# Latent attention of one layer: the order of block 0's key squares, the latent reads and block 1's query transpositions

## The chip, the cores and the metric

The kernel runs on one core of a Trainium2 chip. The metric is device time in microseconds (us), the median of several executions. The core has a matrix engine (TensorE, PE in the rows), a vector engine (VectorE, DVE), a scalar engine (ScalarE, ACT), a general engine (GpSimd, POOL) and a sequencer that issues transfers (SyncE, SP). Each works through its own queue in order; they wait for each other by semaphores. TensorE multiplies out of on-chip memory (SBUF) into accumulation banks (PSUM), which VectorE and ScalarE read here.

## The reference, cut to what matters

The network computes, for 256 tokens of width 1024: feed-forward, SSM layer, feed-forward, feed-forward, **latent attention**, feed-forward, short convolution, and a stick-breaking attention. All is float32; the kernel multiplies large matrices as three products of high and low parts. Only the latent attention is touched here:

```python
def mla_mixer(h, positions, w_in, q_a_norm, kv_a_norm, w_q_b, w_kv_b, q_norm, k_norm, w_out):
    proj = h @ w_in                                      # 384 + 256 + 32 columns
    cq   = rms_norm(proj[..., :Q_LORA], q_a_norm)
    ckv  = rms_norm(proj[..., Q_LORA:Q_LORA + KV_LORA], kv_a_norm)
    k_rope = proj[..., Q_LORA + KV_LORA:]
    q  = (cq @ w_q_b).reshape(b, s, 16, 64 + 32)         # queries
    kv = (ckv @ w_kv_b).reshape(b, s, 16, 64 + 64)       # keys and values
    ...                                                  # rms_norm of q_nope, q_rope, k_nope, k_rope
    q_rope, k_rope = apply_rope(...)                     # rotation by position
    o = causal_block_attention(q_nope, q_rope, k_nope, k_rope, v)   # blocks of 128 queries
    return o.reshape(b, s, 16 * 64) @ w_out
```

## The kernel before, in words

Tokens stand in two blocks of 128 (`tb` 0 and 1). Weights come in units of up to 128 x 2048 elements through a ring of four slots: SyncE loads a unit when the low part of the unit four before it is done (`lo_ready`), ScalarE rounds its high part (`w_hi`, L1297), VectorE subtracts for the low part (`w_lo`, L1864), TensorE multiplies. `split_to(n)` in an engine's program does all units up to n at this place of its queue; `split_half` does half of a low part (L1882). In the latent attention `u0` is the first unit: u0+6 and u0+7 hold the key/value weights, u0+8 to u0+11 the output weights, and u0+12 on belong to the next layer.

The stages of each block are these. `block(...)` (L950) is a product of one 512-column stretch into one accumulation bank; banks are used in turn, so a block waits until the one four before it is read (`claim`). ScalarE reads the query banks (`read_q`) and squares them (`square_q`), VectorE sums the squares (`q_means`), ScalarE takes the root (`root`), VectorE inverts and scales (`inverse`, `scale_q`); GpSimd rotates the last 32 columns of each head (`rotate`), the last two steps behind the squares. Keys and values are read into `kv_tok` (`read_kv`, on ScalarE, two of them on VectorE), squared (`square_k`), summed (`k_means`), and GpSimd takes a power of the sums (L2655) and scales the keys (L2656). `means_ready` counts VectorE's sums in their order.

Then TensorE transposes queries and keys, four heads at a time (`token_turn`, a "turn"; L618 in the rows). All turns of the layer are numbered by the list `MLA_TURNS` and use two banks alternately, so a turn waits until the turn two before it has been copied out (`claim_turn`); `read_turn` on ScalarE or VectorE is this copy. A round of attention (`mla_round`) is four heads of block 0 or two of block 1: `scores` (L1022, with a mask L1024), `tops` (the maximum, VectorE), `exps` (ScalarE), `weights_turn` and its copy `read_weights`, `values` (L1041), `out_norm` (VectorE), and per two rounds an output turn (`out_turn`), whose high and low parts feed the output product.

The order of all this is written out by hand, one list for each engine, and the engines' lists have to agree. Before, TensorE turned all eight groups of queries and then the four key groups of block 0 ahead of `scores(0)`.

## Time and profile before

| | us |
|---|---|
| median of 3 runs | 1321.52 |
| lowest, highest | 1317.18, 1322.16 |
| the profiled execution | 1323.06 |
| its span, first to last instruction | 1321.3 |
| TensorE busy in it | 1292.5 |
| VectorE busy | 767.4 |
| ScalarE busy | 681.8 |
| GpSimd busy | 120.5 |

The part of the latent attention that the change touches lies at about 843 to 882 us of the span. The mean granted clock of TensorE over the span was 0.993 of full speed. A busy share is the time in which an engine has an instruction under way; a row of a timeline begins with its start in us from the span's start and its duration, "x8" is eight instructions merged, and the bracket is the time for which the engine stood still before it and who ended that.

### The profile page before, as it was taken

How to read it: one execution, taken by the hardware profiler on the slowest of the kernel's cores; microseconds unless marked ns; L12 is line 12 of the kernel's file. 1: busy time of each engine (PE TensorE's matmuls, PEld its weight loads, DVE VectorE, ACT ScalarE, POOL GpSimd, SP SyncE). 2: the span in 40 equal slices, each digit the busy share in tenths (PEclk: the TensorE clock that was granted, in tenths of full speed). 3: DMA queues.
4: the chain of work that ended last, by engine and by line, in shares of the span. 5: the costliest groups of instructions: out<-in, count | busy, mean ns of one | idle time of the engine just before them, and what ended most of it. 6: DMA issues, size and time to landing. Idle time of an engine off the chain costs nothing.

```text
span 1321.3 us, 18338 instructions
## 1 busy us (share of the span) xinstructions
PE 1292.5 (98%) x6930; PEld 1103.6 (84%) x6930; DVE 767.4 (58%) x912; ACT 681.8 (52%) x926; POOL 120.5 (9%) x198
## 2 busy tenths in 40 slices
PE   8999999999999999999999999989999999999997
PEld 6888889999778888888888888778888888998895
DVE  5555645778676555554555544865655545766663
ACT  6454435678775544442544534854645434443552
POOL 3000000007630000000000001620000000000000
PEclk9999999999899999999999999999999999999999
DMA  9556645543227455565555563423556564766401
GB/s 295 191 190 207 212 142 191 161 159 96 96 96 254 153 187 181 183 219 160 190 179 183 180 211 120 144 64 96 186 178 198 186 225 125 194 190 223 157 4 48
DMA packets 180478, 219.81 MB, mean 166 GB/s; under 512 B 8666, under 2 KB 132895, under 8 KB 180415
## 3 DMA queue, kind: packets, MB, share of 16 engines
q1 hardware_dynamic: 179438, 218.01, 50.7%
q8 instruction: 42, 0.69, 0.2%
q10 hardware_dynamic: 688, 0.79, 0.2%
q0 software_dynamic: 288, 0.15, 0.1%
q14 instruction: 22, 0.17, 0.0%
HBM read 217.87 MB, written 1.05 MB: 166 GB/s over the span
## 4 chain that ended last, share of the span: by engine, by line
PE 88%; DVE 6%; ACT 5%; issue 1%; DMA 0%; SPq 0%; DVEq 0%; POOLq 0%; ACTq 0%; POOL 0%
PE acc L601 27%; PE acc L603 26%; PE acc L602 26%; PE tr L618 3%; DVE w_lo L1864 2%; ACT w_hi L1297 1%; PE tr L903 1%; PE aux L1041 1%; PE acc L1022 1%; ACT xT_hi L1310 1%; DMA raw<-in_ffn_w_gate 0%; ACT R_hi L1496 0%; DVE zn L2412 0%; PE acc L1238 0%; DVE zr L2411 0%
## 5 line engine op out<-in xcount | busy, mean ns | idle before, releaser
L1864 DVE TENSOR_TENSOR w_lo<-raw,w_hi 128x2048 fp32r<-128x2048 f32 (+1 forms) x196 | 440.7, 2276 | 180.4 <-ACT w_hi L1297 180.3
L1297 ACT ACTIVATE w_hi<-raw 128x2048 fp32r<-128x2048 f32 (+1 forms) x198 | 369.2, 1899 | 118.9 <-PE acc L603 118.1
L601 PE MATMUL acc<-w_hi,xT_hi 128*128 128x512 f32 (+1 forms) x914 | 363.4, 398 | 4.5 <-DVE w_lo L2472 2.8
L603 PE MATMUL acc<-w_hi,xT_lo 128*128 128x512 f32 (+1 forms) x914 | 355.7, 389 | 0.0
L602 PE MATMUL acc<-w_lo,xT_hi 128*128 128x512 f32 (+1 forms) x914 | 355.2, 389 | 0.0
L601 PEld LDWEIGHTS acc<-w_hi,xT_hi 128*128 128x128 f32 x914 | 172.3, 189 | 40.3 <-issue 4.9
L603 PEld LDWEIGHTS acc<-w_hi,xT_lo 128*128 128x128 f32 x914 | 172.2, 188 | 36.4
L602 PEld LDWEIGHTS acc<-w_lo,xT_hi 128*128 128x128 f32 x914 | 172.5, 189 | 33.2
L601 PE MATMUL acc<-w_hi,hT_hi 128*128 128x512 f32 x448 | 175.8, 392 | 0.4 <-DVE y_sb L2382 0.4
L603 PE MATMUL acc<-w_hi,hT_lo 128*128 128x512 f32 x448 | 174.5, 390 | 0.0
L602 PE MATMUL acc<-w_lo,hT_hi 128*128 128x512 f32 x448 | 174.4, 389 | 0.0
L601 PE MATMUL acc<-xT_hi,w_hi 128*128 128x256 f32 (+1 forms) x592 | 167.1, 283 | 1.2 <-DVE w_lo L1864 0.6
L602 PE MATMUL acc<-xT_lo,w_hi 128*128 128x256 f32 (+1 forms) x592 | 165.9, 281 | 0.0
L603 PE MATMUL acc<-xT_hi,w_lo 128*128 128x256 f32 (+1 forms) x592 | 165.9, 281 | 0.0
L2007 DVE SCALAR_TENSOR_TENSOR h<-acc,rstd,sg 128x256 f32<-128x256 f32 x88 | 38.6, 479 | 165.8 <-ACT sg L1400 165.8
L1400 ACT ACTIVATE sg<-acc,rstd 128x256 f32<-128x256 f32 x88 | 37.0, 472 | 181.9 <-PE acc L603 181.8
L601 PEld LDWEIGHTS acc<-xT_hi,w_hi 128*128 128x128 f32 (+1 forms) x592 | 112.2, 190 | 2.0 <-issue 1.8
L602 PEld LDWEIGHTS acc<-xT_lo,w_hi 128*128 128x128 f32 (+1 forms) x592 | 112.2, 190 | 0.3
L603 PEld LDWEIGHTS acc<-xT_hi,w_lo 128*128 128x128 f32 (+1 forms) x592 | 112.2, 190 | 0.0
L2533 POOL TENSOR_SCALAR mean_square<-square_sum 128x1 f32<-128x1 f32 x18 | 5.0, 275 | 1040.4 <-ACT junk L1347 574.0
L601 PEld LDWEIGHTS acc<-w_hi,hT_hi 128*128 128x128 f32 x448 | 84.1, 188 | 17.8 <-DVE y_sb L2382 0.8
L603 PEld LDWEIGHTS acc<-w_hi,hT_lo 128*128 128x128 f32 x448 | 84.1, 188 | 17.8
(294 smaller groups left out, 1140.7 us busy)
## 6 DMA issues: line engine op xcount, KB each, us to landing
raw<-in_ffn_w_down SPq DMA_DIRECT2D x88, 512.0 KB, 4.7
raw<-in_ffn_w_gate SPq DMA_DIRECT2D x87, 512.0 KB, 4.2
raw<-in_ffn_w_up SPq DMA_DIRECT2D x87, 512.0 KB, 5.6
raw<-in_ssm_w_in SPq DMA_DIRECT2D x48, 512.0 KB, 4.7
raw<-in_w_in_a SPq DMA_DIRECT2D x64, 256.0 KB, 4.0
raw<-in_ssm_w_out SPq DMA_DIRECT2D x16, 512.0 KB, 4.0
raw<-in_mla_w_out SPq DMA_DIRECT2D x8, 512.0 KB, 4.6
raw<-in_w_out_a SPq DMA_DIRECT2D x8, 512.0 KB, 4.8
```

What stands on the lines that cost most here:

```text
L601: pe.matmul(o, lh, rh, start=start, stop=False, skip_group_check=skip)
L602: pe.matmul(o, lh, rl, start=False, stop=False, skip_group_check=skip)
L603: return pe.matmul(o, ll, rh, start=False, stop=stop, skip_group_check=skip)
L618: last = pe.transpose(tr[0:n, k % 2, at:at + P], src, ident[:])
L903: last = pe.matmul(tr[:, k % 2, tb * GW + r * HP:tb * GW + (r + 1) * HP], E[:, tb, r * P:(r + 1) * P], xdt[:, g % 2, tb, r * HP:(r + 1) * ...
L1022: pe.matmul(o[:, j * w:(j + 1) * w], qT[0:QK, h0 + j, tb * P:(tb + 1) * P], kT[0:QK, h0 + j, 0:w], start=j == 0, stop=False, skip_group_ch ...
L1041: last = pe.matmul(aux[:, r % 2, j * (VD + 1):(j + 1) * (VD + 1)], pT[:, r % 2, at:at + P], kv_tok[:, kb, h0 + j, NOPE:], start=kb == 0, s ...
L1297: inst = act.activation(w_hi[:, u % RING, 0:n], raw[:, u % RING, 0:n], ACT.Copy)
L1310: inst = act.activation(dst, tr[:, k % 2, at:at + P], ACT.Copy, scale=scale)
L1400: act.activation(sg[:, tb, :], bank(p0 + n, tb)[:, 0:CW], ACT.Silu, scale=rstd[:, tb:tb + 1]).then_inc(gated, 1)
L1864: inst = dve.tensor_tensor(w_lo[:, u % RING, 0:n], raw[:, u % RING, 0:n], w_hi[:, u % RING, 0:n].bitcast(F32), ALU.subtract)
L2007: acc_free(dve.scalar_tensor_tensor(h[:, tb, :], bank(p0 + n, tb)[:, CW:2 * CW], rstd[:, tb:tb + 1], sg[:, tb, :], ALU.mult, ALU.mult), p0 ...
```

## The change

Six things change, all in the latent attention. (1) ScalarE reads all eight key/value banks; VectorE's `read_kv` is gone. (2) ScalarE does the high part of unit u0+8 before the key/value reads, then block 0's key squares, then block 1's query squares (the query squares stood first before, the key squares eleven steps later). VectorE sums block 0's key squares ahead of block 1's query squares, GpSimd finishes block 0's keys before it copies block 1's rotated keys, and the numbers that they wait for in `means_ready` follow. (3) TensorE turns block 0's queries between block 1's key/value blocks, has no turns of block 1's queries there, starts `scores(0)` behind the third key turn, and turns block 1's queries behind the four rounds of scores: two before the weights' turns, one after `values(0)`, one after `values(1)`. (4) The third query turn of block 1 is copied by ScalarE instead of VectorE. (5) VectorE's low part of unit u0+8 is done in two halves, around `out_norm(0)`. (6) ScalarE's high part of unit u0+9 stands behind `read_weights(2)`, ahead of the read of the last query turn.

```diff
--- before.py
+++ after.py
@@ -147,9 +147,9 @@
 SUM_PAIR = (19, 20)
 MLA_TURNS = {name: n for n, name in enumerate(
     [("p", tb, j) for tb in range(TB) for j in range(2)]
-    + [("q", tb, quad) for tb in range(TB) for quad in range(4)]
+    + [("q", 0, quad) for quad in range(4)]
     + [("k", 0, quad) for quad in range(4)]
-    + [("t", 0), ("t", 1), ("t", 2), ("k", 1, 0), ("k", 1, 1), ("o", 0), ("k", 1, 2), ("k", 1, 3), ("t", 3), ("o", 1),
+    + [("q", 1, 0), ("q", 1, 1), ("t", 0), ("t", 1), ("q", 1, 2), ("t", 2), ("q", 1, 3), ("k", 1, 0), ("k", 1, 1), ("o", 0), ("k", 1, 2), ("k", 1, 3), ("t", 3), ("o", 1),
        ("o", 2), ("t", 4), ("o", 3), ("t", 5), ("t", 6), ("o", 4),
        ("t", 7), ("t", 8), ("o", 5), ("t", 9), ("t", 10), ("o", 6), ("t", 11), ("o", 7)])}
 
@@ -1005,9 +1005,9 @@
                         inst = block(u0 + 6 + m // 2, 10 + 4 * tb + m, tb, 3, 2, True, True, 512, both,
                                      at=512 * (m % 2), stride=1024)
                         inst.then_inc(unit_used if tb and m % 2 else mla_part, 1)
-                        if tb:
-                            token_turn("q", m // 2, 2 * (m % 2))
-                            token_turn("q", m // 2, 2 * (m % 2) + 1)
+                        if tb and m in (1, 2):
+                            token_turn("q", 0, 2 * (m - 1))
+                            token_turn("q", 0, 2 * (m - 1) + 1)
 
                 def scores(r):
                     tb, h0, nh = mla_round(r)
@@ -1068,15 +1068,22 @@
                     out_part(n, tb, 0)
                     out_part(n, tb, 1)
 
-                for quad in range(4):
-                    token_turn("k", 0, quad)
-                for r in range(4):
+                token_turn("k", 0, 0)
+                token_turn("k", 0, 1)
+                token_turn("k", 0, 2)
+                scores(0)
+                token_turn("k", 0, 3)
+                for r in range(1, 4):
                     scores(r)
+                token_turn("q", 1, 0)
+                token_turn("q", 1, 1)
                 weights_turn(0)
                 weights_turn(1)
                 values(0)
+                token_turn("q", 1, 2)
                 weights_turn(2)
                 values(1)
+                token_turn("q", 1, 3)
                 token_turn("k", 1, 0)
                 token_turn("k", 1, 1)
                 out_turn(0)
@@ -1614,7 +1621,10 @@
 
                 def read_kv(tb, m):
                     p, b = mla_bank(10 + 4 * tb + m)
-                    act.wait_ge(mla_part, 10 + m // 2 if tb else 6 + m)
+                    if tb and m % 2:
+                        act.wait_ge(unit_used, u0 + 7 + m // 2)
+                    else:
+                        act.wait_ge(mla_part, 10 + m // 2 if tb else 6 + m)
                     act.wait_ge(lat_rstd, tb + 1)
                     acc_free(act.activation(kv_tok[:, tb, 4 * m:4 * m + 4, 0:NOPE + VD], heads(bank(p0 + p, b), 4),
                                             ACT.Copy, scale=lrs[:, tb, 1:2]), p0 + p, b)
@@ -1623,12 +1633,12 @@
                     for m in range(4):
                         p, b = mla_bank(10 + 4 * tb + m)
                         acc_done(act, p0 + p, b)
-                    act.wait_ge(means_ready, tb + 1)
+                    act.wait_ge(means_ready, 2 * tb + 1)
                     act.activation(squares[:, tb, :, 0:NOPE], kv_tok[:, tb, :, 0:NOPE], ACT.Square)\
                         .then_inc(k_squared, 1)
 
                 def root(tb):
-                    act.wait_ge(means_ready, tb + 1)
+                    act.wait_ge(means_ready, 2 * tb + 1)
                     act.activation(qrs[:, tb], qss[:, tb], ACT.Sqrt).then_inc(roots_ready, 1)
 
                 def read_turn(kind, tb, quad):
@@ -1688,33 +1698,34 @@
                 root(0)
                 read_q(1, 1)
                 read_q(1, 2)
+                split_to(u0 + 9)
+                for m in range(4):
+                    read_kv(0, m)
+                square_k(0)
                 square_q(1)
-                read_kv(0, 0)
-                read_kv(0, 1)
-                read_kv(0, 2)
-                split_to(u0 + 9)
-                read_kv(0, 3)
+                read_kv(1, 0)
                 read_turn("q", 0, 0)
                 read_turn("q", 0, 1)
+                read_kv(1, 1)
                 root(1)
-                read_kv(1, 0)
                 read_turn("q", 0, 2)
                 read_turn("q", 0, 3)
-                square_k(0)
                 read_kv(1, 2)
-                read_turn("q", 1, 1)
-                split_to(u0 + 10)
+                read_kv(1, 3)
+                read_turn("k", 0, 0)
                 square_k(1)
-                read_turn("q", 1, 3)
-                read_turn("k", 0, 0)
                 read_turn("k", 0, 2)
                 exps(0)
                 exps(1)
+                read_turn("q", 1, 1)
+                exps(2)
                 read_weights(0)
-                exps(2)
+                read_turn("q", 1, 2)
+                exps(3)
                 read_weights(2)
+                split_to(u0 + 10)
+                read_turn("q", 1, 3)
                 read_turn("k", 1, 0)
-                exps(3)
                 out_high(0)
                 read_turn("k", 1, 2)
                 exps(4)
@@ -2223,13 +2234,6 @@
                                       qrs[:, tb, 1, :].unsqueeze(2).to_broadcast([P, MH, ROPE]), ALU.mult)\
                         .then_inc(q_scaled, 1)
 
-                def read_kv(tb, m):
-                    p, b = mla_bank(10 + 4 * tb + m)
-                    dve.wait_ge(unit_used, u0 + 7 + m // 2)
-                    dve.wait_ge(lat_rstd, tb + 1)
-                    acc_free(dve.tensor_scalar(kv_tok[:, tb, 4 * m:4 * m + 4, 0:NOPE + VD], heads(bank(p0 + p, b), 4),
-                                               lrs[:, tb, 1:2], None, ALU.mult), p0 + p, b)
-
                 def read_turn(kind, tb, quad):
                     k = k0 + MLA_TURNS[kind, tb, quad]
                     dve.wait_ge(turned, k + 1)
@@ -2287,22 +2291,21 @@
                 split_to(u0 + 8)
                 inverse(0)
                 scale_q(0)
+                k_means(0)
                 q_means(1)
                 inverse(1)
                 scale_q(1)
-                k_means(0)
-                read_kv(1, 1)
-                split_to(u0 + 9)
+                read_turn("k", 0, 1)
+                tops(0)
+                k_means(1)
+                read_turn("k", 0, 3)
+                for r in range(1, 4):
+                    tops(r)
                 read_turn("q", 1, 0)
-                read_kv(1, 3)
-                read_turn("q", 1, 2)
-                k_means(1)
-                read_turn("k", 0, 1)
-                read_turn("k", 0, 3)
-                for r in range(4):
-                    tops(r)
                 read_weights(1)
+                split_half(u0 + 8, 0)
                 out_norm(0)
+                split_half(u0 + 8, 1)
                 out_norm(1)
                 read_turn("k", 1, 1)
                 out_low(0)
@@ -2648,10 +2651,9 @@
                 for tb in range(TB):
                     rotate(tb)
                 for tb in range(TB):
-                    pool.wait_ge(means_ready, tb + 1)
+                    pool.wait_ge(means_ready, 2 * tb + 1)
                     link(pool.tensor_copy(k_tok[:, tb, :, NOPE:], kr[:, tb, :].unsqueeze(1).to_broadcast([P, MH, ROPE])))
-                for tb in range(TB):
-                    pool.wait_ge(means_ready, tb + 3)
+                    pool.wait_ge(means_ready, 2 * tb + 2)
                     link(pool.tensor_tensor(krs[:, tb], kss[:, tb], minus_half[:, 0:MH], ALU.pow))
                     pool.tensor_tensor(k_tok[:, tb, :, 0:NOPE], kv_tok[:, tb, :, 0:NOPE],
                                        krs[:, tb, :].unsqueeze(2).to_broadcast([P, MH, NOPE]), ALU.mult)\
```

## Rows read from the trace of the kernel before

**Rows 1.** The page of the profile, its first part: busy time of TensorE.

```profile
...
PE 1292.5 (98%) x6930; PEld 1103.6 (84%) x6930; DVE 767.4 (58%) x912; ACT 681.8 (52%) x926; POOL 120.5 (9%) x198
...
```

**Rows 2.** Timeline of TensorE around block 1's keys (start, duration, form, [idle before <-releaser]).

```profile
...
848.32 0.39 PE L602 MATMUL acc<-w_lo,xT_hi 128*128 128x512 f32 x1
848.54 0.39 PE L603 MATMUL acc<-w_hi,xT_lo 128*128 128x512 f32 x1
849.99 1.08 PE L618 MATMUL tr<-ident,q_tok 128*96 128x128 f32 x8 [1.06 <-DVE q_tok L2222]
...
855.40 1.08 PE L618 MATMUL tr<-ident,q_tok 128*96 128x128 f32 x8 [0.71 <-DVE q_tok L2222]
...
860.29 1.05 PE L618 MATMUL tr<-ident,q_tok 128*96 128x128 f32 x8 [2.41 <-DVE qT L2238]
861.80 0.64 PE L618 MATMUL tr<-ident,k_tok 128*96 128x128 f32 x4 [0.46 <-POOL k_tok L2656]
...
864.77 1.06 PE L1022 MATMUL acc<-kT,qT 96*128 96x128 f32 x8
...
```

**Rows 3.** Timeline of TensorE, from the first weights' product to the first output turn.

```profile
...
870.50 1.11 PE L1041 MATMUL aux<-kv_tok,pT 128*128 128x65 f32 x8 [0.25 <-ACT pT L1662]
...
874.34 0.41 PE L618 MATMUL tr<-ident,o_tok 128*128 128x128 f32 x2 [0.43 <-ACT kT L1641]
...
```

**Rows 4.** Timeline of ScalarE, 843 to 872 us.

```profile
...
843.87 1.49 ACT L1613 ACTIVATE squares<-q_tok 128x1536 f32<-128x1536 f32 x1
845.27 1.83 ACT L1619 ACTIVATE kv_tok<-acc,lrs 128x512 f32<-128x512 f32 x3
...
857.01 1.90 ACT L1297 ACTIVATE w_hi<-raw 128x2048 fp32r<-128x2048 f32 x1
860.99 1.07 ACT L1627 ACTIVATE squares<-kv_tok 128x1024 f32<-128x1024 f32 x1 [2.08 <-DVE kv_tok L2230]
861.97 0.58 ACT L1639 ACTIVATE qT<-tr 96x512 f32<-96x512 f32 x1
862.48 0.68 ACT L1641 ACTIVATE kT<-tr,kcol 96x512 f32<-96x512 f32 x1
...
869.85 0.60 ACT L1662 ACTIVATE pT<-tr 128x512 f32<-128x512 f32 x1 [0.79 <-PE tr L618]
870.35 1.14 ACT L1653 ACTIVATE pm<-acc,nbias 128x128 f32<-128x128 f32 x4
...
```

**Rows 5.** Timeline of VectorE, 847 to 867 us.

```profile
...
847.08 1.71 DVE L2219 TENSOR_TENSOR q_tok<-q_tok,qrs 128x1024 f32<-128x1024 f32 x1
...
849.86 1.21 DVE L2195 TENSOR_REDUCE qss<-squares 128x16 f32<-128x1024 f32 x1
...
853.52 1.23 DVE L2219 TENSOR_TENSOR q_tok<-q_tok,qrs 128x1024 f32<-128x1024 f32 x1
...
855.27 1.21 DVE L2203 TENSOR_REDUCE kss<-squares 128x16 f32<-128x1024 f32 x1
...
866.08 0.69 DVE L2248 TENSOR_REDUCE nbias<-acc 128x4 f32<-128x512 f32 x1 [0.36 <-PE acc L1024]
...
```

**Rows 6.** Timeline of GpSimd, 844 to 862 us.

```profile
...
844.18 0.74 POOL L2644 TENSOR_TENSOR q_tok<-t 128x256 f32<-128x256 f32 x1
...
849.35 1.19 POOL L2644 TENSOR_TENSOR q_tok<-t 128x256 f32<-128x256 f32 x1
850.60 0.61 POOL L2652 COPY k_tok<-kr 128x512 f32<-128x512 f32 x1
...
856.84 2.91 POOL L2655 TENSOR_TENSOR krs<-kss,minus_half 128x16 f32<-128x16 f32 x1 [4.14 <-DVE kss L2204]
859.83 1.92 POOL L2656 TENSOR_TENSOR k_tok<-kv_tok,krs 128x1024 f32<-128x1024 f32 x1
...
```

**Rows 7.** A pause in the SSM layer: timeline of TensorE.

```profile
...
354.89 1.22 PE L879 MATMUL tr<-state,CT 128*128 128x256 f32 x2 [2.61 <-ACT ys L1467]
...
```

**Rows 8.** Windows (busy us of each engine, granted clock PEclk) after that pause.

```profile
...
354.00:366.00 12.00, 11.11 (x38) 9.69 (x39) 5.29 (x11) 5.61 (x13) 8.23 (x12) 0.57 0.24 87
...
```

## The prediction

> **What bounds the kernel now.** First the page's busy times: TensorE is busy 1292.5 us of a span of 1321.3 us [rows 1], so nothing outside TensorE's own queue can give more than the 28.8 us in which it stands still, and a change that only reorders work can move only what lies around the waits of its own stretch. Next the timeline of TensorE in that stretch. The latent attention's pauses are in the brackets of [rows 2]: 1.06 us before block 0's first query turns, 0.71 us before block 1's first, 2.41 us before block 1's last (it waits for VectorE to have emptied the transposition bank), 0.46 us for GpSimd's scaled keys. Later ones are in [rows 3]: 0.25 us before the first weights' product at 870.50, 0.43 us before the first output turn at 874.34. From that turn on the order of all four engines is the same before and after, so I carry the sum to that point, 874.34 us, and hand its shift on to the end unchanged: between there and the end of the layer each step waits for one of the round before it, and no transfer sets a pace.
>
> The profiled execution took 1323.06 us, 1.76 us around its span and 1.54 us above the median of the three runs, 1321.52. I add the shift to both: the sum is against 1323.06, the forecast is about the median.
>
> **Part 1: up to block 0's first key turn.** ScalarE, first. After the last query read it now does the high part of unit u0+8 (1.90 us) [rows 4], which used to stand after three of the key/value reads: 843.67 to 845.5. Three reads at 0.61 us (three in 1.83) bring it to 847.4; the fourth waits for its block, which TensorE ends near 847.6, and is over at 848.3. Then block 0's key squares (1.07) to 849.5, and only then block 1's query squares, which stood at 843.87 (1.49): they end at 850.9, 5.5 us later than before. Who waits for these? GpSimd's last two rotation steps of block 1.
>
> VectorE scales block 0's queries from 847.08. Its first operation took 1.71 us while GpSimd rotated block 1's queries beside it; the same operation for block 1, with GpSimd idle, took 1.23 [rows 5]. GpSimd must now wait there, so I take 1.4 and 0.6 us for the two (bounds 1.23 and 1.71 for the first): done at 849.1, 0.8 us before the 849.9 at which TensorE's wait ended [rows 2]. Block 0's key sums (1.21 and a small step, 1.4 in all) [rows 5] run 849.55 to 850.95, and block 1's query sums (1.21 for the large part [rows 5], 0.9 estimated for the half as large one and the two small steps) to 853.05.
>
> GpSimd, in order: last rotation steps from 851.05. The row of one is 0.74 us when VectorE does something else and 1.19 us when VectorE scales beside it [rows 6]; VectorE reduces here, so I take 0.74 (bounds 0.74 and 1.19 each, 0.9 us together). To 852.5; the copy of the rotated keys 0.61; the power 2.91; the scaling 1.92 [rows 6]: block 0's keys are ready at 858.2, TensorE turns them from 858.3. In the trace of before that is 861.80 [rows 2]. **Gain here: 3.5 us.** Note what limits it: not the key squares, which are 4.4 us earlier on ScalarE, but the squares of the queries put behind them, which hold GpSimd's queue.
>
> TensorE meanwhile: the block that ended its issue at 848.77 (the last matmul at 848.54, one each 0.23 us) [rows 2] is followed at once by the next (six, 1.4 us), eight turns of queries (0.85 us, no wait now: their scaling is done at 849.1), a block (1.5), eight turns with 0.3 us of wait for ScalarE's reads, and the last block, drained at 854.9. Then nothing until 858.3: one pause of 3.4 us in place of 1.06, 0.71, 2.41 and 0.46.
>
> **Part 2: from there to the first weights' product.** Before: 861.80 to 870.50, 8.70 us. Now: two key turns and, when ScalarE has emptied the bank of the first (0.68) [rows 4], the third: 1.95 us to the first scores. Four rounds of scores at 1.12 us (eight matmuls of 1.06 with the mask behind) [rows 2] and the fourth key turn, 0.45: 4.93 us. The last round waits 0.35 us: VectorE reads the fourth key turn only behind the first maximum (0.69) and block 1's key sums (1.21) [rows 5]. Two query turns 0.86 us, at 866.4; the weights' turn then wants the bank that VectorE empties behind the last maximum, at 867.0: 0.75 us of wait. Two weights' turns, 0.9 us. The product waits for ScalarE's copy of the first (0.60) [rows 4], 0.7 us. Sum 1.95 + 4.93 + 0.35 + 0.86 + 0.75 + 0.9 + 0.7 = 10.45 us: the product starts at 868.75 instead of 870.50. **Loss 1.75, left of the gain 1.75 us.**
>
> **Part 3: to the first output turn.** Before: 870.50 to 874.34, 3.84 us [rows 3]. Now two query turns stand in between (0.45 each), and the banks alternate through ScalarE. The third query turn is done at 870.4; behind it ScalarE's queue holds: its read (0.58), the fourth round's exponentials (1.14), the third weights' copy (0.60), the high part of unit u0+9 (1.90), the fourth query read (0.58), the first key read of block 1 (0.68) [rows 4]. Overlaps of 0.1 taken off, that is 5.05 us and ends at 875.45; the output turn needs this last bank and starts at 875.6, 1.25 us later than 874.34. The 1.9 us of u0+9 stood at 857.01 [rows 4], in a pause of TensorE; now they stand before two reads that TensorE waits for, while ScalarE idles from 855.6 to 858.9. TensorE waits 0.75 us before block 1's first key turn and 1.7 us before its second. 3.84 becomes 6.85: **loss 3.0 us.**
>
> Sum: -3.5 + 1.75 + 3.0 = +1.25 us. Costed at nothing: the reads that moved from VectorE to ScalarE (0.61 us each, over at 855.6, before 858.9); VectorE's low part of unit u0+8, now two halves around the first normalisation (VectorE waits for the products there; if that cover were gone, 1.2 us before the output's o_tok, which has 4 us); SyncE's load of unit u0+12, which waits for that low part and is issued some 12 us later: only loads of later units are queued behind it, and its data is wanted after the last output turn. GpSimd's chain for block 1's keys starts at 863.8 and takes 4.9 us [rows 6], done at 868.7, wanted at 872.7. Bounds of the sum: -1.75 if the part of unit u0+9 costs nothing after all (with the product 0.5 us earlier, -2.3); +1.25 with GpSimd's 0.9 and 0.5 us of handovers, +2.7. I take +1.25, since each term is a row of a like operation.
>
> **TensorE's clock.** The trace has a pause that shows the price: in the SSM layer TensorE stood still 2.61 us [rows 7], and the stretch 354 to 366 us had a mean granted clock of 0.57 with TensorE busy 11.11 of 12 us [rows 8]: at 1.2 instead of 2.4 GHz for 12 x 0.43 / 0.5 = 10.3 us, up to 5.1 us lost. The pause of 2.41 us in the latent attention [rows 2] cost nothing of the kind. The three runs lie 5.0 us apart (1317.18 to 1322.16), about one such fall, so I read the median as a run with one fall somewhere. The new pause of 3.4 us is longer than both. In it a fall costs: 10.3 us at half clock from about 858, where of the work about 4.5 us doubles less 0.3 us of waits that absorb it: 4.2 us.
>
> The Trainium skill, "TensorE: Matmul & The Clock Gate", Part 1: The HAM clock gate, says that TensorE's clock is gated to half once it has been idle long enough and is given back only after sustained work. By that rule the change would turn three short pauses, of which the trace shows none punished, into one that is, and the time would come out at the rival's; by the row alone it is open. The trace agrees with the rule at one pause and not at another of nearly the same length.
>
> **The rivals.**
> A. *The clock falls once more than before, in the new pause.* For: the length, and two shorter waits of 0.75 and 1.7 us later that invite a second chance. Against: falls at pauses of this size are chance, and before had one of 2.41 us there, so its median may already pay. 1321.52 + 1.25 + 4.2 = 1327.0.
> B. *The earlier product counts and the tail is not paid* (it decides at the first output turn: within 873 us). The 1.9 us of u0+9 would have to fall in time that TensorE has other work. For: only two reads lie behind it. Against: ScalarE works in order, and both banks alternate. 1321.52 - 1.75 = 1319.8; with luck of the clock (no fall), 1317.
> C. *Slower beyond doubt:* both pauses fall, the one at 855 and the one at 872 to 875 us, where TensorE works 0.5 us in 3. It decides when the second comes after the clock has risen again. 4.2 + 5 us: 1321.52 + 1.25 + 9.2 = 1332.
> D. The order has no effect on the end at all: 1321.5, inside the forecast's own range; I give it no share apart.
>
> **How the numbers follow.** Forecast (shift +1.25, falls as before) 0.46, A 0.28, B 0.19, C 0.07. Time of the likeliest: 1321.52 + 1.25 = 1322.8 us; its own range 1321 to 1325. The range for eight in ten takes in A and most of B: 1318.5 to 1328.0. A measurement can tell about 0.5%, 6.6 us, from no change: under 1314.9 needs B with more gain than TensorE's waits in the stretch allow, 0.03; over 1328.1 is C and the upper edge of A, 0.10; the rest 0.87.
>
> **What would show it.** Timeline after: block 0's first key turn at 858.3 (gain 3.5), one bracket of about 3.4 us before it; the first weights' product at 868.75; the releaser of the wait before block 1's second key turn is ScalarE's read of the last query turn, which starts behind a w_hi of 1.9 us; the first output turn at 875.6. The granted clock in the stretch 856 to 870 tells the forecast from A. I am wrong if the output turn comes before 874.3, or if the run's end differs from it.

## The result, and the profile after

| | before | changed |
|---|---|---|
| median, us (12 runs each) | 1322.16 | 1325.61 |
| lowest, highest | 1317.18, 1322.99 | 1323.39, 1326.79 |
| ratio, 95% interval | | 1.0034 [1.0023, 1.0044] |
| profiled execution, span | 1323.06, 1321.3 | 1323.48, 1321.7 |

The change makes the kernel 0.34% slower (3.5 us between the medians, 4.3 between the means of 1321.0 and 1325.3). That is less than the 0.5% that the prediction took as the least a measurement can tell, but the interval leaves out 1: slower it is. It lies inside the stated range, 1318.5 to 1328.0, 2.8 us above the forecast of 1322.8 and just above that forecast's own range, 1321 to 1325. Of e1's 11 runs below, one took 1607.82 us at a granted clock of 0.749 and is left out of every number. TensorE's busy time on the page did not move: 1292.3 against 1292.5 us [rows 1].

```profile
...
span 1321.7 us, 18339 instructions
...
PE 1292.3 (98%) x6930; PEld 1104.2 (84%) x6930; DVE 767.4 (58%) x910; ACT 682.6 (52%) x929; POOL 121.4 (9%) x198
...
```

In the stretch, every time below is counted from the first query product of block 0, since the two executions reach it 6 us apart. That is this row of the kernel before, and then the same one of the changed kernel (timeline of TensorE):

```profile
...
829.08 0.43 PE L601 MATMUL acc<-w_hi,xT_hi 128*128 128x512 f32 x1
...
```

```profile
...
823.04 0.43 PE L601 MATMUL acc<-w_hi,xT_hi 128*128 128x512 f32 x1
...
```

The next fence is TensorE's timeline of the changed kernel, and answers to [rows 2] and [rows 3].

```profile
...
852.54 3.02 PE L618 MATMUL tr<-ident,k_tok 128*96 128x128 f32 x12 [3.74 <-POOL k_tok L2658]
...
864.96 1.11 PE L1041 MATMUL aux<-kv_tok,pT 128*128 128x65 f32 x8 [0.53 <-ACT pT L1672]
...
868.77 0.61 PE L618 MATMUL tr<-ident,k_tok 128*96 128x128 f32 x4 [0.56 <-ACT pT L1672]
871.05 0.73 PE L618 MATMUL tr<-ident,k_tok 128*96 128x128 f32 x4 [1.67 <-ACT qT L1649]
871.63 0.66 PE L618 MATMUL tr<-ident,o_tok 128*128 128x128 f32 x2
...
878.84 1.11 PE L1041 MATMUL aux<-kv_tok,pT 128*128 128x65 f32 x8 [0.95 <-DVE pT L2260]
...
```

Read against 823.04, block 0's first key turn comes at 29.50 (before: 861.80 - 829.08 = 32.72), the first weights' product at 41.92 (41.42), the first output turn at 48.59 (45.26), the fourth weights' product at 55.80 (50.94). One pause of 3.74 us has taken the place of four, and a new one of 1.67 us ends with ScalarE's read of the last query turn. From the fourth weights' product to the first turn of the next layer's hidden values it is 62.58 us in both traces, so the 4.9 us of the stretch reach the next layer whole.

Why the spans still differ by only 0.4 us: in this execution the SSM layer's pause of [rows 7] was there again, 2.60 us, and cost nothing. From the turn behind it to the first query product it takes 469.48 us here (353.56 to 823.04) and 474.19 in the kernel before (354.89 to 829.08): the fall there had cost 4.7 us. First its row, then its windows (columns as in [rows 8]):

```profile
...
353.56 0.70 PE L879 MATMUL tr<-state,CT 128*128 128x256 f32 x2 [2.60 <-ACT ys L1474]
...
```

```profile
...
350.00:360.00 10.00, 7.40 (x48) 6.48 (x47) 6.47 (x9) 6.99 (x20) 9.68 (x11) 1.00 0.32 105
...
```

The granted clock is 1.00 where [rows 8] had 0.57. Near the end it is the other way round: a pause of 1.41 us at 1289.31 had no fall behind it in the kernel before (1.42 us at 1290.49, granted clock 1.00 from 1280 to 1300), and has one here:

```profile
...
1280.00:1300.00 20.00, 18.59 (x97) 13.52 (x97) 6.65 (x8) 11.71 (x17) 0.00 (x0) 0.91 0.00 1
...
```

From the fourth weights' product to the end of the span it is 441.28 us before and 442.86 here, 1.6 us more. In the executions of e1 to e11 it is 441.2 to 441.4 in nine and 443.1 and 442.9 in the two (e5, e9) whose clock fell at that place; with no fall there the end follows the stretch. One profiled execution of each kernel therefore compares two draws of the clock, and says little on 4 us. In the latent attention the windows of the changed kernel are:

```profile
...
850.00:852.00 2.00, 0.00 (x0) 0.00 (x0) 0.72 (x2) 0.00 (x0) 1.92 (x2) 0.73 0.00 0
852.00:854.00 2.00, 1.46 (x7) 1.40 (x8) 0.00 (x0) 0.33 (x1) 1.04 (x2) 0.50 0.00 0
...
856.00:858.00 2.00, 2.00 (x11) 1.70 (x11) 0.27 (x1) 1.56 (x2) 0.00 (x0) 0.56 0.00 0
858.00:860.00 2.00, 2.00 (x20) 1.96 (x18) 1.97 (x4) 1.14 (x4) 0.10 (x1) 1.00 0.00 0
...
870.00:872.00 2.00, 0.94 (x6) 0.79 (x7) 0.18 (x1) 1.49 (x3) 0.00 (x0) 0.85 1.01 345
872.00:874.00 2.00, 2.00 (x12) 1.99 (x11) 1.00 (x2) 0.38 (x1) 0.00 (x0) 0.50 0.45 152
874.00:876.00 2.00, 2.00 (x13) 1.78 (x12) 0.00 (x0) 0.68 (x1) 0.00 (x0) 0.79 0.00 0
876.00:878.00 2.00, 1.89 (x14) 1.46 (x12) 1.67 (x4) 0.00 (x0) 0.00 (x0) 1.00 0.00 0
...
```

TensorE's clock is at 1.2 GHz from 851, inside the first pause, to nearly 858 (6.8 us), and again from just behind the second to nearly 875 (3.4 us). What is order and what is clock had to be separated by runs.

ScalarE's and GpSimd's rows confirm the chain of part 1 and the queue of part 3. GpSimd waits 2.36 us for the query squares, and then takes its rotation (0.75), power (2.91) and scaling (2.21):

```profile
...
845.07 0.75 POOL L2646 TENSOR_TENSOR q_tok<-t 128x256 f32<-128x256 f32 x1 [2.36 <-ACT squares L1620]
...
847.29 2.91 POOL L2657 TENSOR_TENSOR krs<-kss,minus_half 128x16 f32<-128x16 f32 x1
850.28 2.21 POOL L2658 TENSOR_TENSOR k_tok<-kv_tok,krs 128x1024 f32<-128x1024 f32 x1
...
```

ScalarE does the weights' copy, the high part of u0+9, the query read and the key read in a row without a gap:

```profile
...
843.46 1.47 ACT L1620 ACTIVATE squares<-q_tok 128x1536 f32<-128x1536 f32 x1
...
868.02 0.60 ACT L1672 ACTIVATE pT<-tr 128x512 f32<-128x512 f32 x1
868.50 1.93 ACT L1304 ACTIVATE w_hi<-raw 128x2048 fp32r<-128x2048 f32 x1
870.30 0.61 ACT L1649 ACTIVATE qT<-tr 96x512 f32<-96x512 f32 x1
870.78 0.71 ACT L1651 ACTIVATE kT<-tr,kcol 96x512 f32<-96x512 f32 x1
...
```

### The profile page after: what moved, and what is told of

Read it like the earlier page. It is cut to its first block, busy times and chain, and to the rows that moved or that the text cites. A ratio compares the mean times of both kernels' runs of the same rounds, so it can differ in the third digit from the quotient of the medians.

```text
span 1321.7 us, 18339 instructions
## 1 busy us (share of the span) xinstructions
PE 1292.3 (98%) x6930; PEld 1104.2 (84%) x6930; DVE 767.4 (58%) x910; ACT 682.6 (52%) x929; POOL 121.4 (9%) x198
## 4 chain that ended last, share of the span: by engine, by line
PE 89%; ACT 5%; DVE 4%; issue 1%; DMA 1%; POOL 1%; SPq 0%; DVEq 0%; POOLq 0%; ACTq 0%
PE acc L601 27%; PE acc L603 27%; PE acc L602 27%; PE tr L618 4%; DVE w_lo L1875 1%; ACT w_hi L1304 1%; DMA raw<-in_ffn_w_up 1%; PE tr L903 1%; PE acc L1022 1%; PE aux L1041 1%; ACT xT_hi L1317 0%; ACT R_hi L1503 0%; PE acc L1245 0%; DVE zn L2415 0%; DVE zr L2414 0%
```

## The experiments

Filling matmuls below are of the form `pe.matmul(aux[:, 0, 0:P], ident[:], ident[:], start=True, stop=True)`; they write a bank that nothing is held in at that time, and nobody reads them; the kernel's own `keep_busy` at its start has the same form. They keep TensorE at work while it waits. Those of the right size change no wait of the kernel; the overfilled ones (e2, e4) push back what follows. The means are over all compared runs; "before" was run beside each of the four groups (changed; e1 to e4; e5 to e8; e9 to e11), with means of 1321.0, 1320.1, 1320.2 and 1319.7. The marks (first key turn, first weights' product, first output turn, fourth weights' product, in us after the first query product) come from the one profiled execution; e4's and e6's are a second and a third trace of the latent attention of before.

| kernel | mean, us | granted clock, mean of runs | ratio to before, 95% | marks |
|---|---|---|---|---|
| before | 1319.7 to 1321.0 | 0.995 | 1 | 32.72, 41.42, 45.26, 50.94 |
| changed | 1325.3 | 0.992 | 1.0034 [1.0023, 1.0044] | 29.50, 41.92, 48.59, 55.80 |
| e1 u0+9 moved back | 1323.5 | 0.993 | 1.0028 [1.0015, 1.0041] | 29.51, 41.01, 46.31, 52.00 |
| e2 first pause overfilled | 1327.7 | 0.992 | 1.0061 [1.0044, 1.0078] | 31.36, 41.82, 48.78, 57.13 |
| e3 query squares first | 1324.5 | 0.992 | 1.0035 [1.0022, 1.0049] | 28.25, 38.75, 45.70, 54.04 |
| e4 before, SSM overfilled | 1319.5 | 0.997 | 0.9994 [0.9984, 1.0004] | 32.73, 42.14, 45.97, 51.66 |
| e5 changed, both pauses filled | 1322.1 | 0.996 | 1.0015 [1.0000, 1.0030] | 29.51, 40.01, 46.69, 52.37 |
| e6 before, SSM filled | 1318.0 | 0.997 | 0.9986 [0.9975, 0.9996] | 32.99, 42.01, 45.85, 51.53 |
| e7 reordered | 1318.1 | 0.996 | 0.9983 [0.9971, 0.9995] | 27.31, 37.81, 43.11, 48.80 |
| e8 reordered, SSM filled | 1316.0 | 0.998 | 0.9968 [0.9957, 0.9978] | 27.35, 37.85, 43.16, 48.84 |
| e9 before, all filled | 1317.5 | 0.997 | 0.9984 [0.9972, 0.9996] | 32.18, 40.89, 44.73, 50.41 |
| e10 changed, all filled | 1319.4 | 0.998 | 1.0000 [0.9989, 1.0011] | 29.51, 40.01, 46.68, 52.37 |
| e11 as e8, VectorE reordered | 1315.5 | 0.998 | 0.9965 [0.9951, 0.9978] | 27.36, 37.57, 42.87, 48.55 |

**e1, the high part of u0+9 moved back.**

```diff
                 read_kv(1, 3)
+                split_to(u0 + 10)
                 read_turn("k", 0, 0)
...
                 read_weights(2)
-                split_to(u0 + 10)
                 read_turn("q", 1, 3)
```

> The changed kernel with ScalarE's high part of unit u0+9 moved from behind the third weights' copy into ScalarE's idle time ahead of block 0's first key read. Theory S (the order costs +1.25 us, of it 3.0 in front of the first output turn through this one operation; the rest of the measured +0.34% is falls of TensorE's clock in the two new pauses): from the first weights' product to the first output turn about 5.0 us instead of 6.7, the pause of 1.7 us before block 1's second key turn goes, and with it the second fall; time 3 to 5 us below the changed kernel's 1325.6, so 1320.5 to 1322.5, ratio to before 0.999 to 1.000. Rival R (the loss is in the new order of turns and scores, not in this operation): 1325 again, ratio 1.003.

The timeline of TensorE in e1:

```profile
...
866.96 1.11 PE L1041 MATMUL aux<-kv_tok,pT 128*128 128x65 f32 x8 [0.52 <-ACT pT L1672]
...
870.78 1.10 PE L618 MATMUL tr<-ident,k_tok 128*96 128x128 f32 x8 [0.56 <-ACT pT L1672]
872.26 0.41 PE L618 MATMUL tr<-ident,o_tok 128*128 128x128 f32 x2 [0.38 <-ACT kT L1651]
...
```

From weights' product to output turn it is 5.30 us, and the pause of 1.67 us is gone: the operation was in the way. The time was not what I wrote: 1323.5 instead of 1320.5 to 1322.5, because the first pause is still there and its fall too. The profiled execution shows it (granted clock 0.83 from 850 to 860 us, and 11.50 us from key turn to product, where e3 and e5 have 10.50): 1.0 us.

**e2, the first pause filled.** Before `token_turn("k", 0, 0)`:

```diff
+                for _ in range(26):
+                    pe.matmul(aux[:, 0, 0:P], ident[:], ident[:], start=True, stop=True)
```

> The changed kernel with 26 matmuls of 128x128, whose result nobody reads, in TensorE's queue in the pause ahead of block 0's first key turn (2.9 us at 2.4 GHz). They change no wait. Theory S (a fall of the clock in that pause is worth 2 to 4 us in most runs): granted clock 1.00 from 848 to 860 us, time 1322 to 1323.5, ratio 1.000 to 1.001, the second fall before the output turn may stay. Rival R (the clock costs nothing on the path, the order alone costs 3.5 us): 1325.6, ratio 1.003.

A miss of my own making. The trace has two instructions for each float32 matmul, and 26 of them took 5.8 us, not 2.9:

```profile
...
852.21 5.96 PE L1072 MATMUL aux<-ident 128*128 128x128 f32 x52
858.01 1.04 PE L618 MATMUL tr<-ident,k_tok 128*96 128x128 f32 x8
...
```

The key turn came 1.86 us late. What can be kept is that it took 10.46 us from there to the product, with the clock at 1.00. The clock fell at the second pause (0.77 from 870 to 885 us), and the time says nothing on either theory. e5 repeats it at the right size.

**e3, block 1's query squares first.**

```diff
                 read_q(1, 2)
+                square_q(1)
                 split_to(u0 + 9)
                 for m in range(4):
                     read_kv(0, m)
                 square_k(0)
-                square_q(1)
```

> The changed kernel with block 1's query squares back at their old place, ahead of the high part of unit u0+8 and the reads of block 0's keys and values. Theory S: GpSimd's rotation is no longer held, block 0's key squares end 1.2 us later but the first key turn comes 1.2 us earlier (at 16.9 instead of 18.1 us after block 1's last query product begins), the pause is about 2.3 us instead of 3.7; time 1 to 2.5 us below the changed kernel, 1323 to 1324.5, ratio 1.001 to 1.002. Rival R2 (the key squares set the first key turn): it comes 1.2 us later, 1326.8, ratio 1.004.

The mark moved as expected, 1.25 us earlier, and the pause shrank to 1.97 us; R2 falls. The time hardly followed: 1324.5 on the mean is at the edge of what was expected, and the ratio, 1.0035, above it. The rows of the one profiled execution say where the gain went there:

```profile
...
855.62 1.08 PE L618 MATMUL tr<-ident,k_tok 128*96 128x128 f32 x8 [1.97 <-POOL k_tok L2658]
...
866.12 1.11 PE L1041 MATMUL aux<-kv_tok,pT 128*128 128x65 f32 x8 [0.52 <-ACT pT L1672]
...
872.22 1.06 PE L618 MATMUL tr<-ident,k_tok 128*96 128x128 f32 x4 [1.67 <-ACT qT L1649]
...
```

```profile
...
870.00:880.00 10.00, 8.33 (x40) 7.21 (x41) 2.27 (x5) 3.71 (x5) 0.00 (x0) 0.66 0.34 107
...
```

The clock fell at the second pause instead, and for long: from the product to the fourth weights' product it takes 15.29 us, against 12.36 in e5, a price of 2.9 us. Only 2 of 10 runs have a high clock (1320.6 and 1321.4 at 0.996 and 0.995; the others are 1324.2 or more at 0.991 to 0.993); at which pause it fell in those that were not profiled is not shown.

**e4, the kernel before with the SSM layer's pause filled.** In its turn ahead of the wait of L879:

```diff
                         elif name == "cb":
+                            if g == 6:
+                                pe.wait_ge(exp_done, 11)
+                                for _ in range(20):
+                                    pe.matmul(aux[:, 0, 0:P], ident[:], ident[:], start=True, stop=True)
                             claim_turn(k)
```

> The kernel before, with 20 matmuls whose result nobody reads in TensorE's 2.6 us pause in the SSM layer (2.2 us). Theory S (the spread of the kernel before, 1317.2 to 1323.0 in 12 runs, is falls of the clock, most of them in this pause, 10.3 us at 1.2 GHz each): the higher runs vanish, median 1317.5 to 1319, ratio 0.997. Rival R3 (the spread comes from elsewhere, as transfers): median stays 1322, ratio 1.000.

The spread narrows from 6.6 us to 2.7 (1318.3 to 1321.0) and the granted clock rises from 0.995 to 0.997, so most of the spread is the clock's at this pause. But 20 fillers took 4.5 us in a pause of 2.6, the same mistake as in e2, and pushed everything back: the gain was eaten, and the mean is above the expected 1317.5 to 1319.

**e5, both pauses of the changed kernel filled at the right size.** 13 fillers as in e2, and:

```diff
                 token_turn("k", 1, 0)
+                pe.wait_ge(o_read, 1)
+                for _ in range(6):
+                    pe.matmul(aux[:, 0, 0:P], ident[:], ident[:], start=True, stop=True)
                 token_turn("k", 1, 1)
```

> The changed kernel with 13 matmuls whose result nobody reads in the pause before block 0's first key turn and 6 before block 1's second key turn (0.223 us each, as 26 of them took 5.8 us: 2.9 and 1.3 us, shorter than the pauses of 3.7 and 1.7 us). No wait moves. Theory S: the clock stays at 2.4 GHz from 845 to 885 us; from the first query product to the first output turn 46.5 us (45.26 before), to the fourth weights' product 52.2 us (50.94 before, 55.8 in the changed kernel's trace): +1.25 us by order; times 1320.5 to 1322, ratio to before 1.000 to 1.001 against 1.0034. Rival R (order alone costs 3.5 us or more): the marks stay near 48.6 and 55, ratio 1.003.

```profile
...
849.15 3.06 PE L1072 MATMUL aux<-ident 128*128 128x128 f32 x26
853.05 1.08 PE L618 MATMUL tr<-ident,k_tok 128*96 128x128 f32 x8 [0.84 <-POOL k_tok L2663]
...
863.55 1.11 PE L1041 MATMUL aux<-kv_tok,pT 128*128 128x65 f32 x8 [0.53 <-ACT pT L1677]
...
869.66 0.61 PE L618 MATMUL tr<-ident,k_tok 128*96 128x128 f32 x4 [0.33 <-ACT qT L1654]
870.23 0.41 PE L618 MATMUL tr<-ident,o_tok 128*128 128x128 f32 x2
...
875.91 1.11 PE L1041 MATMUL aux<-kv_tok,pT 128*128 128x65 f32 x8 [0.95 <-DVE pT L2265]
...
```

This is the changed order with TensorE's clock at 2.4 GHz throughout the stretch. The marks are 29.51, 40.01, 46.69 and 52.37. Against 50.94 before it is +1.43 us, where the prediction had +1.25. The time is 1322.1, 3.2 us below the changed kernel on no change but the fillers (2.4 us when each is set against the mean of before that ran beside it). R falls as a whole, though the mean is just above the expected window and the runs still spread from 1318.7 to 1325.0; with the SSM layer's pause filled too (e10) the spread is 3.8 us instead of 6.3.

**e6, the kernel before with the SSM layer's pause filled at the right size** (11 in place of e4's 20).

> The kernel before with 11 matmuls whose result nobody reads in the SSM layer's 2.6 us pause (2.45 us; with 20 they took 4.4 us and pushed the work behind them by 1.8 us). Theory S: no fall in that pause, nothing pushed; median 1317.3 to 1318.3, ratio 0.998; what spread is left comes from the latent attention and the end. Rival R3 (the clock isn't it): 1320.7 with the old spread.

```profile
...
350.00:360.00 10.00, 9.86 (x69) 8.94 (x68) 6.47 (x9) 7.00 (x23) 9.68 (x12) 1.00 0.31 105
...
```

As expected: 1316.8 to 1319.0, mean 1318.0, TensorE busy 9.86 us in 350 to 360, where the unfilled pause leaves 7.40. R3 falls. A kernel that was not to be touched there gets 2 us out of eleven useless matmuls.

The traces of e4 and e6 show one thing more. Neither filled the pause of 2.41 us in before's own latent attention [rows 2], and in both the clock fell behind it. First e4, then e6:

```profile
...
859.09 3.84 PE L618 MATMUL tr<-ident,k_tok 128*96 128x128 f32 x16 [0.46 <-POOL k_tok L2660]
...
860.00:870.00 10.00, 9.74 (x69) 8.51 (x69) 6.06 (x11) 6.54 (x16) 4.82 (x2) 0.86 0.17 60
...
```

```profile
...
855.01 1.75 PE L618 MATMUL tr<-ident,q_tok 128*96 128x128 f32 x8 [2.42 <-DVE qT L2242]
...
850.00:860.00 10.00, 7.12 (x38) 5.36 (x39) 8.31 (x11) 5.66 (x7) 6.50 (x3) 0.83 0.34 106
...
```

Their fourth weights' products come at 51.66 and 51.53 instead of 50.94, so such a fall cost 0.7 and 0.6 us; the first trace of before had drawn none there.

**e7, ScalarE's queue reordered.**

```diff
                 read_q(1, 2)
-                split_to(u0 + 9)
+                square_q(1)
                 for m in range(4):
                     read_kv(0, m)
                 square_k(0)
-                square_q(1)
+                split_to(u0 + 9)
...
                 read_weights(2)
-                split_to(u0 + 10)
                 read_turn("q", 1, 3)
                 read_turn("k", 1, 0)
                 out_high(0)
                 read_turn("k", 1, 2)
+                split_to(u0 + 10)
                 exps(4)
```

> The changed kernel with ScalarE's queue in another order: block 1's query squares first, then the reads of block 0's keys and values, the key squares, then the high part of unit u0+8; the high part of unit u0+9 only ahead of the fifth round's exponentials, where ScalarE waits 2.7 us anyway. Theory S: first key turn 27.2 us after the first query product (29.5 in the changed kernel, 32.7 before), first weights' product 37.7, first output turn 43.0, fourth weights' product 48.7 against 50.94: -2.2 us by order, pause before the first key turn about 1.1 us, few falls of the clock there. Times 1317 to 1319, ratio 0.997 to 0.999. Rival R (turning block 1's queries between the rounds costs 3 us whatever ScalarE does): 1323.

```profile
...
854.51 1.08 PE L618 MATMUL tr<-ident,k_tok 128*96 128x128 f32 x8 [1.33 <-POOL k_tok L2658]
...
865.01 1.11 PE L1041 MATMUL aux<-kv_tok,pT 128*128 128x65 f32 x8 [0.53 <-ACT pT L1672]
...
870.31 0.41 PE L618 MATMUL tr<-ident,o_tok 128*128 128x128 f32 x2 [0.38 <-ACT kT L1651]
...
876.00 1.11 PE L1041 MATMUL aux<-kv_tok,pT 128*128 128x65 f32 x8 [0.95 <-DVE pT L2260]
...
```

The marks are within 0.11 us of the expected ones: -2.14 us to the fourth weights' product. The rival, that turning block 1's queries between the rounds costs whatever ScalarE does, falls: the idea of the change is a gain once ScalarE's two weight operations stand where TensorE waits for neither and the query squares come first again.

**e8, the same with e6's fillers.**

> The kernel of the run before with the 11 filling matmuls in the SSM layer's pause as well. Theory S: both gains add, -2.2 us by order and no fall in the SSM layer: median 1315 to 1316.5, ratio 0.995 to 0.997. Rival R3: as the run before.

Mean 1316.0, 1314.5 to 1317.5: 0.32% faster than the kernel before, 0.66% than the changed one. Against e6, which has the same fillers and ran beside it, it is 2.0 us less.

**e9, the kernel before with its own latent-attention pause filled too.** Ahead of `token_turn("q", 1, 2)` at m == 3:

```diff
+                            if m == 3:
+                                for _ in range(9):
+                                    pe.matmul(aux[:, 0, 0:P], ident[:], ident[:], start=True, stop=True)
```

> The kernel before with 11 filling matmuls in the SSM layer's pause and 9 (2.0 us) in its 2.41 us pause ahead of block 1's last query turns. Theory S: the falls left in the run with the SSM pause alone filled (mean 1318.0) go: mean 1317.0 to 1317.6. It is the clock-free time of the kernel before, for the next run. Rival: 1318.1, no fall was left to remove.

1317.5, at the upper end of what was expected. Against e6's 1318.0, run on another chip, 0.6 us is no clear difference (standard errors 0.3 and 0.2), but it is the size of the two falls seen in e4 and e6.

Its trace starts the stretch 0.6 us sooner than the three of before (32.18 to the first key turn against 32.72, 32.73 and 32.99), and not by the clock: the first query turns wait 0.41 us for VectorE's scaled queries, where [rows 2] have 1.06.

```profile
...
843.42 1.08 PE L618 MATMUL tr<-ident,q_tok 128*96 128x128 f32 x8 [0.41 <-DVE q_tok L2229]
...
```

**e10, the changed kernel with all three pauses filled** (e5 and e6 together).

> The changed kernel with its two pauses and the SSM layer's filled (13, 6 and 11 matmuls). Theory S: what stays against the run above is the order alone, 1.25 to 1.45 us: mean 1318.4 to 1319.2, and from there to the changed kernel's 1325.3 is the clock (6 us, of it 2 to 3 in the SSM layer). Rival R (an effect of the change outside the stretch): over 1320.

1319.4, a little above the window. Beside e9 in the same comparison it is the order's price in time: 1319.41 - 1317.46 = 1.95 us, standard error 0.44 from the two spreads, at the same granted clock (0.998 and 0.997). By the marks of these two traces it is 52.37 - 50.41 = 1.96 us; against the first trace of before it was 1.43, and the 0.5 us between the two is e9's earlier start. From 1319.4 to the changed kernel's 1325.3 is the clock: 5.9 us.

**e11, VectorE reordered on top of e8.**

```diff
                 tops(0)
-                k_means(1)
                 read_turn("k", 0, 3)
-                for r in range(1, 4):
-                    tops(r)
+                tops(1)
+                k_means(1)
+                tops(2)
                 read_turn("q", 1, 0)
+                tops(3)
```

> The reordered kernel with the SSM fill, and on VectorE the fourth key read ahead of block 1's key sums, these behind the second maximum, and the first query read of block 1 ahead of the fourth maximum. By the rows: the 0.2 us wait of the last scores and the 0.6 us wait of the first weights' turn go; first key turn to first weights' product 9.8 instead of 10.5 us; time 0.5 to 0.8 us less than 1316.0: mean 1315.3. Rival: the fourth exponentials come later and ScalarE takes it back, 1316.0 or more.

From key turn to product 10.21 us instead of 10.50, not 9.8. The wait of the last scores is gone (0.20 us in e5), but the first weights' turn still waits 0.44 us for the read of the query turn (0.60 in e8), and the product waits 0.69 us for the copy of the weights (0.53 in e8). Mean 1315.5 against 1316.0 on another chip, ratio 0.9965 against 0.9968: the trace has 0.3 us, the times can't tell it. It is the fastest of the thirteen kernels, if by nothing certain over e8.

## Why the prediction was right or wrong

**Part 1 (gain 3.5): right.** First key turn predicted at 858.3, that is 29.22 after the first query product; measured 29.50. That it was held by GpSimd behind the query squares, e3 showed by undoing it (-1.25). The 0.3 us are GpSimd's scaling, 2.21 instead of 1.92 us. It takes 2.21 in the changed kernel, e1, e5 and e10, where VectorE still scales queries beside its beginning, and 1.92 in e7 and e11, where it does not; I had counted such a bound for the rotation only.

**Part 2 (10.45): right.** Measured 10.50 with the clock undisturbed (e3, e5). The three waits that it named are there, each some 0.2 us shorter: 0.20, 0.59 and 0.53 us for 0.35, 0.75 and 0.7.

**Part 3 (3.84 becomes 6.85): right in the sum,** 6.68 in e5. The text made the one operation of u0+9 look like nearly the whole of it; e1 and e5 split it: 1.4 us by that operation (6.68 to 5.30), 1.5 us is left for the two query turns and their reads. So rival B's condition, that u0+9 costs nothing, would never have given the whole -1.75: with it moved, the stretch is level with before (1.43 - 1.38 = 0.05 us; 0.6 by e9's marks), no gain.

**The sum by order, +1.25: right in sign, and 0.2 to 0.7 us too small:** +1.43 and +1.96 by the marks, against two traces of before, and 1.95 with an error of 0.44 by time. The shift reached the end, as stated, except for the fall near 1291, which is the clock's.

**"Falls as before": this step failed,** and it carried the highest chance. None of the changed kernel's 12 runs has a mean granted clock over 0.994, while before has runs at 0.997 and 0.998. Rival A, put at 0.28, is what happened, with a smaller price. I had 4.2 us for a fall in the long pause, worked out from 10.3 us at half clock behind it. In the changed kernel's trace the slow time was 6.8 us, 1.6 of it inside the pause, and the price 1.92 us (12.42 against 10.50 us from key turn to product); in e1 it was 1.0. The fall at the second pause cost 1.52 (13.88 against 12.36 to the fourth weights' product), and 2.9 in e2 and e3, where it lasted longer. Together 3.4 us, and 1.43 + 3.4 is the 4.9 of the trace. That both fall in one execution was rival C's picture, at 0.07 and 9.2 us: the picture was right, the price nearly three times too high. In the SSM layer, where TensorE hardly waits behind the pause (busy 11.11 of 12 us, [rows 8]), the 10.2 us at half clock did cost 4.7.

The other half of the step was the 2.41 us pause of before, read as free from its one trace: e4 and e6 have a fall there, at 0.7 and 0.6 us.

Over all runs: changed less filled is 5.9 us (e10), before less filled is 2.3 to 2.7 us (means 1319.7 to 1320.2 less 1317.5, e9), so the change added 3.2 to 3.6 us of clock to 1.4 to 2.0 us of order, some 5 us, where the comparison of the two kernels had 4.3 on the means (1325.3 - 1321.0); the parts come from other chips than the whole, and the difference of about 1 us stays open. How the clock's part divides over the pauses is known only for the profiled executions. That the time came out inside the stated range owes something to the width that A gave it.

**The rule of the Trainium skill** ("TensorE: Matmul & The Clock Gate", Part 1: The HAM clock gate) spoke against the change, and should have had the weight of the forecast: by the page's rule TensorE's clock drops after idleness. The runs side with the page: both traces that keep the whole first pause have a fall there (changed, e1), and fillers alone take 3.2 us off the changed kernel (e5).

The profile had one pause of 2.61 us with a fall and one of 2.41 without. I took the median of three runs as "one fall somewhere" and did not ask how often a pause half as long again would be hit.

## What to carry to other kernels

Count TensorE's pauses, not only their sum: several short ones that become one long one can leave the path alone and still cost some us, by the half clock of the work behind it (1.0 to 1.9 us here). Price such a fall from the work that TensorE does in the slow time, not from the slow time itself: where it waits anyway, little is lost. Before a weight operation is moved, see what stands behind it in its engine's queue at the new place: here 1.9 us moved out of idle time and in front of two reads cost 1.4 us and opened a second pause. And to tell order from clock, fill the pause with matmuls nobody reads, of a length taken from a measured one, in both kernels, and compare marks from a common row; one trace of each is not enough.

## What the runs showed of the hardware

A float32 matmul with 128 moving columns is two instructions in the trace and takes 0.223 us at 2.4 GHz (26 in 5.80 us, e2); a transposition of the same size is one, and takes about 0.11 (eight in 1.03 us and four in 0.60, e5).

Most of the spread of this kernel goes with TensorE's clock. Over 124 runs (the changed kernel, e1 to e8, and the 26 of before beside e1 to e4), each 0.001 of granted clock less goes with 0.94 us more (least squares with an own level for each kernel; 0.7 us is left as scatter). With the SSM layer's pause filled the spread is 2.2 to 3.8 us (e4, e6, e8 to e11), where before has 5.8 to 7.1.

A pause of 2.6 us can have a fall behind it in one execution and none in another ([rows 7, 8] and the changed kernel's row at 353.56). Seven profiled executions have the SSM layer's pause unfilled. From the turn behind it to the first query product they take 474.2 us (before, e7, with 10.2 us at half clock), 472.7 to 472.8 (e1, e2, e3, with 6.8) and 469.5 (the changed kernel and e5, with none); the six filled ones take 469.4 to 469.5. So a fall there cost 4.7 or 3.3 us, and five of seven had one.

VectorE's half of a low part took 2.95 us instead of 1.21 when GpSimd's scaling started 0.05 us ahead of it (e11; VectorE, then GpSimd):

```profile
...
862.11 2.95 DVE L1897 TENSOR_TENSOR w_lo<-raw,w_hi 128x1024 fp32r<-128x1024 f32 x1
...
865.52 1.21 DVE L1897 TENSOR_TENSOR w_lo<-raw,w_hi 128x1024 fp32r<-128x1024 f32 x1
...
```

```profile
...
862.06 1.92 POOL L2663 TENSOR_TENSOR k_tok<-kv_tok,krs 128x1024 f32<-128x1024 f32 x1
...
```

The Trainium skill, "GPSIMD Engine Reference", section 1 (Specifications), has GpSimd's SBUF interfaces shared with VectorE, with contention when VectorE has two SBUF inputs; this operation has two such inputs (the weights and their high part), and the rows agree: VectorE's 1.74 us more are nearly GpSimd's 1.92. It hit nothing on the path here.
